# Reordering four engines' queues around the SwiGLU stages of a two-layer encoder: products joined before weight sums, low parts split three products ahead, entry loads before the x store

## The reference

```
for l in range(2):
    h = rms(x, attn_norm[l]); z = h @ w_in[l]
    x = x + concat(diff_attention(z), latent_attention(z)) @ w_o[l]
    h = rms(x, ffn_norm[l])
    x = x + (silu(h @ w_gate[l]) * (h @ w_up[l])) @ w_down[l]     # d_ff = 2816
return rms(x, final_norm)
```

## Time and profile before

| | us |
|---|---|
| median of 3 runs (2365.97 to 2375.09) | 2370.06 |
| the profiled execution, its own time | 2371.45 |
| its span | 2369.6 |
| TensorE busy | 2269.2 |
| VectorE busy | 1772.6 |
| GpSimd busy | 975.5 |
| ScalarE busy | 973.8 |

### The profile page before, as it was taken

One profiled execution on the slowest core, in us unless ns is written; L12 is line 12 of the kernel. 1 busy time (PEld: TensorE's weight loads), 2 busy tenths in 40 slices (PEclk: granted clock), 3 DMA queues, 4 the chain that ended last, 5 costly groups with the idle time before them and its releaser, 6 DMA issues.

```text
span 2369.6 us, 31240 instructions
## 1 busy us (share of the span) xinstructions
PE 2269.2 (96%) x10600; PEld 1880.4 (79%) x10600; DVE 1772.6 (75%) x2794; ACT 973.8 (41%) x1876; POOL 975.5 (41%) x689
## 2 busy tenths in 40 slices
PE   8999999989999999899999999999899999989997
PEld 6888888878777777778788888888788888877876
DVE  6988388877767666988658873887867666688876
ACT  4555145534443443433224550455343343343331
POOL 4314000125667666688510010001245454566882
PEclk9999999999999999999999999999999999999998
DMA  8624541333656555844233135313322323275421
GB/s 298 223 90 156 192 157 65 107 138 110 223 195 225 205 196 212 291 156 134 98 111 121 60 116 202 140 63 115 112 89 98 111 97 111 89 260 204 145 71 72
DMA packets 93463, 346.89 MB, mean 146 GB/s; under 512 B 9760, under 2 KB 9888, under 8 KB 74016
## 3 DMA queue, kind: packets, MB, share of 16 engines
q1 hardware_dynamic: 92624, 344.53, 41.6%
q10 hardware_dynamic: 720, 0.86, 0.1%
HBM read 237.35 MB, written 108.00 MB: 146 GB/s over the span
## 4 chain that ended last, share of the span: by engine, by line
PE 79%; DVE 10%; issue 3%; ACT 1%; DMA 1%; POOL 1%; DVEq 0%; SPq 0%; ACTq 0%; POOLq 0%
PE bank L519 25%; PE bank L521 25%; PE bank L520 25%; PE bank L1155 2%; DVE u L2164 1%; PE bank L993 1%; DMA raw<-in_wffn 1%; DVE made L2146 1%; DVE made L2136 1%; PE bank L1001 1%; DVE s_stage L2108 1%; POOL acc L873 1%; DVE raw L2109 1%; PE bank L526 1%; PE bank L525 1%
## 5 line engine op out<-in xcount | busy, mean ns | idle before, releaser
L893 POOL TENSOR_TENSOR slot<-raw,slot 128x512 fp32r<-128x512 f32 x160 | 230.6, 1444 | 307.1 <-ACT slot L1601 307.0
L519 PE MATMUL bank<-h_hi,slot 128*128 128x512 f32 x640 | 254.6, 398 | 20.5 <-ACT snap L1611 20.5
L521 PE MATMUL bank<-h_hi,slot 128*128 128x512 f32 x640 | 253.7, 396 | 0.0
L520 PE MATMUL bank<-h_lo,slot 128*128 128x512 f32 x640 | 253.0, 395 | 0.0
L519 PE MATMUL bank<-u,slot 128*128 128x512 f32 x560 | 223.8, 400 | 28.0 <-DVE x L2200 23.5
L870 POOL TENSOR_TENSOR acc<-sq,zero 128x512 f32<-128x512 f32 x6 | 6.7, 1116 | 565.2 <-ACT sq L1392 565.2
L520 PE MATMUL bank<-u,slot 128*128 128x512 f32 x560 | 222.1, 397 | 0.0
L521 PE MATMUL bank<-u,slot 128*128 128x512 f32 x560 | 221.9, 396 | 0.0
L519 PE MATMUL bank<-h_hi,w 128*128 128x512 f32 x512 | 205.1, 401 | 0.0
L521 PE MATMUL bank<-h_hi,w 128*128 128x512 f32 x512 | 201.2, 393 | 0.0
L520 PE MATMUL bank<-h_lo,w 128*128 128x512 f32 x512 | 200.8, 392 | 0.0
(11 more groups left out here) (255 smaller groups left out, 5897.3 us busy)
## 6 DMA issues: line engine op xcount, KB each, us to landing
w<-parked SPq DMA_DIRECT2D x81, 1024.0 KB, 4.8
raw<-in_wffn SPq DMA_DIRECT2D x112, 512.0 KB, 3.3
u_kept<-made SPq DMA_DIRECT2D x148, 256.0 KB, 2.1
uf<-u_kept SPq DMA_DIRECT2D x70, 512.0 KB, 4.7
parked<-w SPq DMA_DIRECT2D x27, 1024.0 KB, 6.3
parked<-p SPq DMA_DIRECT2D x27, 1024.0 KB, 4.9
raw<-in_watt SPq DMA_DIRECT2D x27, 512.0 KB, 4.5
praw<-in_watt SPq DMA_DIRECT2D x27, 512.0 KB, 5.8
```

The source lines that it names most:

```text
L519: nc.tensor.matmul(out_ap, lhs[0], rhs[0], start=first, stop=False, skip_group_check=joins)
L520: nc.tensor.matmul(out_ap, lhs[0], rhs[1], start=False, stop=False, skip_group_check=joins)
L521: return nc.tensor.matmul(out_ap, lhs[1], rhs[0], start=False, stop=last, skip_group_check=joins)
L893: nc.gpsimd.tensor_tensor(slot[i][:, 1, :], gate_source(i), slot[i][:, 0, :].bitcast(F32), ALU.subtract).then_inc(s_gate_lo.sem, 1)
```

## The change

No arithmetic changes. What moves:

1. **Gate stage, DVE.** `gate_sums` goes behind `gate_joined` and `silu_scaled` of batch 0. `made_sums` of a pair goes from its end into the first tile of the next pair, behind `gate_sums` (`sums_of`). The loop runs over (second tile, next first tile).
2. **Gate stage, SP.** The stores of the sums (`keep_sums`) go with them, to behind the first load of the next pair.
3. **Layer 0, preps.** Of the three roundings of attention weights a pair, ACT does one after S2 in the first tile, one after A11 and one before S3 in the second (before: after S1, after S1, after S3). POOL and SP follow.
4. **FFN entry.** All four chunk loads stand ahead of the x store; ACT rounds chunks 2 and 3 behind all squares; two of the four `t3_made` go behind the square root.
5. **Down projection.** u is rounded and its low parts are made three products ahead (`U_AHEAD`) instead of seven; `last_tile` makes those of G1, G5 and G2 only. `residual_sums` and `made_sums` of the last pair go to `added(0, G4)`. POOL makes the low part of G1 ahead of the weight sums. Buffers of u for odd groups change places, and SP's loads follow. The low parts of the plain u (`plain_u_lo`) go to N3 and G6 of the last group, two each, instead of one each at G1, G5, G2 and G4.
6. **End.** `SUMS_BEFORE` is 6; six instead of four additions stand ahead of the root.

```diff
-ENTRY_ROUNDS = [3, 5, 6, 7]
+ENTRY_ROUNDS = [3, 5]
-SUMS_BEFORE = 4
+SUMS_BEFORE = 6
+U_AHEAD = 3
...
@@ SP, ffn_entry
-                for j in range(RAW):
+                for j in range(GCH):
                     sp.wait_ge(s_lo.sem, s_lo.step_at(l, 0, j - RAW))
                     load_raw(l, 0, j)
                 keep_x(l, 1)
-                for j in range(RAW, GCH):
-                    ...
@@ SP, gate_up_loads: after load_gate(l, c, 1, c + 1, 0)
+                if c > 1:
+                    keep_sums(l, c - 1)
                 if prep:
                     next_prep(prep_at(c, 0))
...
                 keep_u(l, c, G1)
+                if prep:
+                    next_prep(prep_at(c, 1))
                 if c < FC - 1:
                     load_gate(l, c + 1, 0, c + 1, 2)
+                    load_up(l, c + 1, 0, c + 1, 3)
@@ SP, down_loads
                 next_u(G2)
+                if d == 0:
+                    sp.wait_ge(s_res.sem, s_res.layer_at(l, 2 * MH - 1))
+                    load_u(l, 1, G4)
+                next_raw(G7, 0)
                 next_u(G4)
-                next_raw(G7, 0)
+                if d == 0:
+                    keep_sums(l, FC - 1)
@@ POOL, down_weights
+                down_lo(l, d, G1)
                 down_sums(l, d)
-                down_lo(l, d, G1)
@@ ACT, entry
+                entry_hi(2)
                 nc.scalar.activation(loaded[:], ones[:, 0:1], ACT.Silu)
+                entry_hi(3)
@@ ACT, down
-                def next_u_hi(d, g):
-                    if d < ND - 1:
-                        u_hi(d + 1, g)
+                def next_u_hi(d, n):
+                    ahead = WP * d + n + U_AHEAD + 1
+                    if ahead < WP * ND:
+                        u_hi(ahead // WP, ahead % WP)
+                    elif ahead == WP * ND:
+                        act.wait_ge(s_u_plain, 4 * 16 * (l + 1))
+                        for m in range(4):
+                            plain_u_hi(m)
@@ DVE
-                def tile(c, tt):
-                    gate_sums(*after(c, tt))
+                def tile(c, tt, sums_of=None):
                     gate_joined(c, tt, 0)
                     silu_scaled(c, 2 * tt)
+                    gate_sums(*after(c, tt))
+                    if sums_of is not None:
+                        made_sums(sums_of)
                     gate_joined(c, tt, 1)
                     silu_scaled(c, 2 * tt + 1)
                     up_joined(c, tt)
-                    if tt:
-                        made_sums(c)
...
+                tile(1, 0)
                 with dve.Fori(1, FC - 1) as c:
-                    tile(c, 0)
                     tile(c, 1)
-                tile(FC - 1, 0)
+                    tile(c + 1, 0, c)
...
                     for group in range(WP):
+                        if d == 0 and group == G4:
+                            residual_sums()
                         added(d, group)
-                        if d == 0 and group == G5:
-                            residual_sums()
-                        if d < ND - 1:
-                            u_lo(d + 1, group)
-                        elif group in (G1, G5, G2, G4):
-                            plain_u_lo(group)
+                        if d == 0 and group == G4:
+                            made_sums(FC - 1)
+                        ahead = WP * d + group + U_AHEAD
+                        if ahead < WP * ND:
+                            u_lo(ahead // WP, ahead % WP)
+                        elif ahead < WP * ND + 2:
+                            plain_u_lo(2 * (ahead - WP * ND))
+                            plain_u_lo(2 * (ahead - WP * ND) + 1)
```

More of the change, by code:

```diff
@@ L1642, in prep_hi, with tile, prep_after @@
                     last.then_inc(s_prep_hi, 1)
-                def tile(c, tt, preps=(None, None)):
+                def tile(c, tt, preps=(None, None, None)):
                     nxt = after(c, tt)
+                    def prep_after(n):
+                        if preps[n] is not None:
+                            prep_hi(preps[n])
                     copied(c, tt, 0)
                     gate_hi(*nxt, A11)
+                    prep_after(0)
                     gate_hi(*nxt, A12)
@@ L1659, in tile @@
                     silu_tile(c, tt, 1)
+                    prep_after(2)
                     gate_hi(*nxt, S3)
-                    if preps[1] is not None:
-                        prep_hi(preps[1])
                 def last_tile(c):
@@ L1698, in _ @@
                 act.wait_ge(s_tr.sem, s_tr.half_at(l, 1, UNITS - 1))
-                for k in range(MH):
-                    t3_hi(k)
+                t3_hi(0)
+                t3_hi(1)
                 silu_plain(0)
+                t3_hi(2)
+                t3_hi(3)
                 t12_hi(0)
@@ L2297, in output @@
                                                ALU.mult).then_inc(s_y, 1)
-            for k in range(4):
+            for k in range(6):
                 down_add(KT + k)
```

100 lines of the change are left out of this document (44 added, 56 removed).

## The result

The changed kernel takes 2283.83 us (median of 4 runs, 2283.13 to 2284.68) against 2368.01 for the kernel before (4 runs, 2365.48 to 2375.09): ratio 0.964, 95% interval 0.9618 to 0.9663. The forecast was 2281 with a range of 2268 to 2302. The profiled execution of the changed kernel took 2283.84 us with a span of 2282.0, against 2371.45 and 2369.6 before: 87.6 us of span are gone, where the sum of the prediction had 89.0.

The account below looks back on a forecast made before the run. TensorE bounds the kernel, with 98.6 us lost around waits. Gains 33.7+22.1+20.6+10.6+2.0 = 89.0 us take the profiled 2371.45 to 2282.4, and 2281 as median (that execution is 1.4 above it); range 2268 to 2302.

Parts of the forecast that it names:

- What bounds the kernel: TensorE; 98.6 us lost to idle time and slow matmuls in layer 0's gate stage, FFN entries and down projections.
- Gate stage: Layer 0: the join, waiting only for A12, lets the copy arrive in time; 34.7 lost less 1 cost, gain 33.7 us.
- Entries: FFN entries: last square no longer stands behind a chunk load, so the sum is ready before TensorE asks; gain 22.1 us.
- First groups of the down projection: Two low parts, not eight, precede the additions; 15.8+14.8 recoverable less 10 for new waits, gain 20.6 us.
- The wait for additions at G7: Down projection, first group: gated sums and a low part ahead of N3's additions make them 1.0 to 3.5 us late.
- the margin at G2: Down projection, first group: additions of G1 end near 978.6 and G2 wants them at 979.6.
- Last group: Down projection: plain u's low parts stand two products later, removing the wait for their rounding; gain 10.6 us, no cost.
- End: Kernel end: two unissued products move ahead and VectorE has two fewer additions behind the root; gain 2.0 us, bounds 0 to 3.
- GpSimd does bind in the down projection: Rival: GpSimd bounds the down projection, 1 us a group and 3 more at each first group; 2295 us, chance 0.17.
- The second raw chunk: Rival: its load comes late in layer 0's gate stage, behind sums and preps; half that gain goes, 2298 us, chance 0.13.
- The slower rival: Gate stage: late weight sums make ScalarE's rounding of S1 hold S3's copy, 5 us in 20 pairs; 2381 us, chance 0.03.
- The rule on shared SBUF interfaces: Gate stage: GpSimd contention makes all eight sums take 14.2 us; second join at 22.5, not 20, still in time; total unchanged.

Follow-up runs that it names:

- the two runs with earlier loads: Changed kernel with the next first weight half's loads issued earlier in the down projection's first group, before the residual sums or at half of them: 2289.60 and 2290.08 us.
- the store first: Changed kernel with SyncE's 2 MB x store at an FFN's entry back ahead of the loads of chunks 2 and 3: 2281.17 us.

## Why the prediction held, by its steps

- **What bounds the kernel.** Right: all but 4.2 of the 87.6 us came from the three places it named, and 2.1 of these from the end. Of its ledger of losses (98.6 us) 13.5 us are left in the down projections and a little at the entries. Its pace of 0.2268 us a matmul holds: 380.8 us for 1680.
- **Gate stage: 33.7 forecast, 35.0 measured.** The forecast cost of 1 us did not arise; no margin that it worked out was used up. But the account of why was half of it. It told the join's place; alone that gives 12.4. It needs the gated sums and their stores moved too, alone worth 5.2 (415.8 to 410.6). And the raw load, which it treated only as a risk to the new order, held VectorE for 34.3 us where the gated sums moved and the weight sums did not.
- **Entries: 22.1 forecast, 20.7 measured.** The mechanism stood: no wait for the sum of squares, none of VectorE for the x store. The miss is 0.7 us an entry; TensorE waits 0.85 and 0.84 us for the root of the norm, for which the prediction had no term. It did not say that the change does it twice, by the store's place and by the rounding's.
- **First groups of the down projection: 20.6 forecast, 16.6 measured** (groups 0 and 1 of both layers in the table above). Its mechanism was right in place and time: it had G5's low parts ready 47.7 us after the stage's start, and they came at 47.6; it had 5 us lost a layer, and 7.2 and 6.3 are above 190.5. The mis-sized part of that term is idle time, 3.7 and 4.1 us for 3.2, and what is lost on top of it, 3.5 and 2.2 us for 1.8. The wait for additions at G7, forecast at 1.0 to 3.5, is 0.38; the margin at G2, forecast at 1.0, is 0.11.
- **Last group: 10.6 forecast, 11.4 measured** (44.4 and 43.3 us to 38.1 twice). Putting VectorE's order back alone costs 12.6, since the wait that returns is 4.70 us and not the 3.36 of the earlier trace rows.
- **End: 2.0 forecast, 2.1 measured** as a stage; not tried apart.
- **Unforeseen, 2.1 us:** 1.7 of it stand ahead of the first FFN, where the diff touches nothing; one profile of each kernel can't tell that from the spread between runs.
- **Luck.** The total came within 2.8 us of the forecast partly because the parts' misses cancel: the first groups and the entries fell short by 5.4, the rest exceeded the forecast by 4.3.
- **The rivals.** GpSimd does bind in the down projection, but in one product of each layer and not in every group: 1.8 and 2.1 us above 190.5 are all that is left with its order changed. The second raw chunk was never waited for. The slower rival did not come; ScalarE's rounding of S1 was in time in every tile.
- **The rule on shared SBUF interfaces.** The prediction set 4.9 us for four weight sums and, by the rule, 14.2 for all eight sums. VectorE's 33.3 us more of busy time in the changed kernel, with no instruction added, is of this kind: 18.1 us of it are the low parts of u and 7.7 the weight sums, both with two SBUF inputs, now made at times when GpSimd works. The Trainium skill, GPSIMD Engine Reference, section 1 (Specifications), names contention where a VectorE instruction has two SBUF inputs; the runs agree for the gated sums (0.69 alone, 1.51 to 1.78 beside GpSimd). In the gate stage this was hidden, as forecast. In the down projection it decided the two runs with earlier loads, and that the prediction had only in its bounds (low parts 1.3 to 3.5 us).

## What to carry to other kernels

Ask of a wait that is left which engine's own queue holds it before asking for earlier data: an earlier load set GpSimd to work beside VectorE and lost more than the 3.35 us, which a swap in GpSimd's queue then won. When several edits serve one wait, undo each alone and together: here one pair was redundant (either sufficed) and one was a conjunction (neither did, and with the gated sums and preps moved but not the weight sums the gate stage took 424.8 us, longer than the 415.8 of the kernel before). Where engines wait in a ring through a buffer, try the instruction that releases the ring ahead of the one that needs the next load, even if the engine has free time: VectorE was busy only 75% of the span in the kernel before.

## What the runs showed of the hardware

- A 128x512 VectorE subtraction of two SBUF tiles takes 0.69 us with GpSimd idle and 1.5 to 1.8 beside it; four of them, moved by nothing but the time of a load, went from 2.7 to 6.5 us. GpSimd's own instructions take 1.29 and 1.75 in the two cases, so both lose.
- One input in PSUM is enough to be spared. In the profile of the changed kernel 376 of VectorE's 735 TENSOR_TENSOR of 128x512 without a bank run at least partly at the same time as one of GpSimd's, and 252 of them last over 0.9 us; of the other 359 none does. Of the 876 that read a bank 517 run beside GpSimd, and none lasts over 0.9 us. The kernel before shows the same (226 of 359, and none of 452).
- It is not only instructions with two SBUF inputs that are slowed. At the entry of the changed kernel, beside GpSimd's split of a chunk, a VectorE multiplication by a column and a small step of the norm's root took 1.49 and 1.07 us; with the store first, where GpSimd was idle at that time, 0.48 and 0.17:

```profile
499.87 1.49 DVE L2059 TENSOR_SCALAR t_tmp<-x,g 128x512 f32<-128x512 f32 x1
...
504.57 1.07 DVE L1843 TENSOR_SCALAR eps_var<-ms 128x4 f32<-128x4 f32 x1
```

```profile
498.66 0.48 DVE L2062 TENSOR_SCALAR t_tmp<-x,g 128x512 f32<-128x512 f32 x1
...
501.21 0.17 DVE L1846 TENSOR_SCALAR eps_var<-ms 128x4 f32<-128x4 f32 x1
```

  The entries are 1.0 to 1.1 us shorter there; that this is the reason is argued, not shown. The section of the Trainium skill named above (GPSIMD Engine Reference, section 1) has contention for a second kind of VectorE instruction too, those in a 2-port performance mode. Whether these two ran in it, no run here shows.
- Of TensorE's clock: behind a wait of 3.35 us the granted clock was 0.50 and then 0.68 in windows of 4 us, and 3.0 us were lost on top of it; behind one of 3.68 us in layer 1 it was 0.65 and then 0.92, and 1.8 us were lost; behind one of 0.68 us it stayed 1.00. So the length of a wait alone does not tell what its clock costs. The nine waits in the gate stage of before cost 20.5 us as waits and 34.7 in all.
